# Expert gates of a two-layer hybrid block: the two parts of a token summed in PSUM by 128-column products

## The reference

```python
def peer_ffn(x, w_query, sub_keys, down, up):
    q = (xt @ w_query).reshape(T, H, 2, PEER_HALF)
    s = jnp.einsum('thcd,cnd->thcn', q, sub_keys).astype(jnp.float32)
    sv, si = lax.top_k(s, K)
    ...
    cand_i = (si[:, :, 0, :, None] * PEER_NKEYS + si[:, :, 1, None, :]).reshape(T, H, K * K)
    top_s, pos = lax.top_k(cand_s, K)
    idx = jnp.take_along_axis(cand_i, pos, axis=-1)
    gate = jax.nn.softmax(top_s, axis=-1)
```

## Time and profile before

| | us |
|---|---|
| median of three runs | 3004.24 |
| lowest and highest | 3000.68, 3005.28 |
| the profiled execution | 3001.47 |
| its span, from the first to the last instruction | 2999.7 |

### The profile page before, as it was taken

One profiled execution on the slowest core, in us unless ns is written; L12 is line 12 of the kernel. 1 busy time (PEld: TensorE's weight loads), 2 busy tenths in 40 slices (PEclk: granted clock), 3 DMA queues, 4 the chain that ended last, 5 costly groups with the idle time before them and its releaser, 6 DMA issues.

```text
span 2999.7 us, 43936 instructions
## 1 busy us (share of the span) xinstructions
PE 2936.4 (98%) x17304; PEld 2595.8 (87%) x17304; DVE 2015.1 (67%) x3109; ACT 1455.8 (49%) x2275; POOL 14.6 (0%) x37
## 2 busy tenths in 40 slices
PE   8999999999999899999999999999999999999998
PEld 6888888889999788888888999988898998888996
DVE  5869998765555586999876655557665556665554
ACT  5531775554444444257545444445455444545443
POOL 0000000000000000000000000000000000000000
PEclk9999999999999999999999999999999999999999
DMA  5334455765545433445567554545555655554553
GB/s 179 110 127 155 157 178 206 256 257 189 196 174 182 137 99 120 155 155 183 197 236 269 199 193 181 197 140 180 182 170 174 188 186 185 172 183 141 154 185 125
DMA packets 223246, 528.52 MB, mean 176 GB/s; under 512 B 13450, under 2 KB 87344, under 8 KB 212080
## 3 DMA queue, kind: packets, MB, share of 16 engines
q1 hardware_dynamic: 221856, 521.11, 50.9%
q0 software_dynamic: 1232, 5.25, 0.5%
HBM read 507.42 MB, written 18.88 MB: 175 GB/s over the span
## 4 chain that ended last, share of the span: by engine, by line
PE 93%; DVE 4%; ACT 1%; DMA 0%; issue 0%; SPq 0%; POOL 0%; DVEq 0%; ACTq 0%; POOLq 0%
PE ps L2235 16%; PE ps L1238 14%; PE ps L2219 12%; PE ps L1288 12%; PE ps L1301 12%; PE ps L1272 11%; PE ps L552 3%; PE ps L561 3%; PE ps L1227 2%; PE ps L2476 1%; DVE ring_lo L535 1%; PE ps L655 1%; PE ps L1050 1%; PE ps L2400 0%; PE ps L2384 0%; PE ps L1213 0%
## 5 line engine op out<-in xcount | busy, mean ns | idle before, releaser
L1886 DVE TENSOR_TENSOR ring_lo<-ring,w_hi 128x1024 fp32r<-128x1024 f32 x320 | 388.7, 1224 | 270.7 <-ACT w_hi L1882 269.5
L1882 ACT ACTIVATE w_hi<-ring 128x1024 fp32r<-128x1024 f32 x320 | 336.7, 1057 | 268.9 <-PE ps L2235 182.3
L1238 PE MATMUL ps<-h_t,ring 128*128 128x256 f32 x2048 | 463.5, 379 | 0.9 <-ACT arena L885 0.9
L1238 PEld LDWEIGHTS ps<-h_t,ring 128*128 128x128 f32 x2048 | 379.0, 190 | 47.5 <-issue 1.3
L1288 PE MATMUL ps<-h_t_lo,down_hi 128*128 128x256 f32 x1024 | 288.2, 281 | 0.0
L1288 PE MATMUL ps<-h_t_expert,down_lo 128*128 128x256 f32 x1024 | 287.8, 281 | 0.0
L1288 PE MATMUL ps<-h_t_expert,down_hi 128*128 128x256 f32 x1024 | 286.8, 280 | 0.0
L2219 PE MATMUL ps<-h_t_hi,w_hi 128*128 128x256 f32 x928 | 260.0, 280 | 2.7 <-ACT arena L2034 2.7
L2219 PE MATMUL ps<-h_t_lo,w_hi 128*128 128x256 f32 x928 | 261.4, 282 | 0.0
L2219 PE MATMUL ps<-h_t_hi,ring_lo 128*128 128x256 f32 x928 | 259.7, 280 | 0.0
L1673 DVE TENSOR_TENSOR up_lo<-ring,up_hi 128x2048 fp32r<-128x2048 f32 x64 | 146.7, 2292 | 99.8 <-ACT up_hi L948 99.8
(11 more groups left out here) (444 smaller groups left out, 6682.9 us busy)
## 6 DMA issues: line engine op xcount, KB each, us to landing
ring<-in_peer_down SPq DMA_DIRECT2D x128, 1024.0 KB, 5.0
ring<-in_w_in SPq DMA_DIRECT2D x140, 512.0 KB, 3.6
ring<-in_peer_up SPq DMA_DIRECT2D x68, 1024.0 KB, 4.7
ring<-in_w SPq DMA_DIRECT2D x132, 512.0 KB, 3.5
ring<-in_peer_up SPq DMA_DIRECT2D x120, 512.0 KB, 4.2
arena<-late_gates SPq DMA_DIRECT2D x16, 1024.0 KB, 6.5
ring<-in_w_out SPq DMA_DIRECT2D x16, 512.0 KB, 3.6
ring<-in_peer_w_query SPq DMA_DIRECT2D x16, 512.0 KB, 4.6
```

Of the source, the lines that this page charges most:

```text
L1238: m = pe.e.matmul(PS[:, act_bank(b), j * T:(j + 1) * T], RING[:, b % 2, j * D + kc * P:j * D + (kc + 1) * P], HT[:, kc, :], start=kc == 0, ...
L1882: a.e.activation(W_HI[:, g % HI_SLOTS, :], RAW[:, g % RAW_SLOTS, :], ACT.Copy).then_inc(*a.count(f"c{g}_hi"))
L1886: v.e.tensor_tensor(RAW_LO[:, g % RAW_SLOTS, :], RAW[:, g % RAW_SLOTS, :], W_HI[:, g % HI_SLOTS, :].bitcast(F32), ALU.subtract).then_inc(* ...
```

## The change

For each token `sums` makes two products of 128 columns into the same 128 columns of PSUM, the high part first (it starts the sum) and the low part onto it. The weights, HOT1 of the token, are the same in both. Four tokens now take one bank, and six banks take turns: GATE_BANKS = (0, 1, 2, 3, 6, 7). ScalarE copies the finished gates (`gates_high` is renamed `gates_out`, and it counts `gates{s}`); `gates_low` on VectorE is gone; whoever waited for `low` waits for `gates`, and a `sums` waits for the one six before.

```diff
-GATE_BANKS = (0, 2, 6)
+GATE_BANKS = (0, 1, 2, 3, 6, 7)
...
-        def gate_sums(s, part, late):
-
-            bank = GATE_BANKS[s % 3]
-            sums = PS[:, bank:bank + 2, :].rearrange("p b (j i n) -> p (b j) i n", i=2, n=P)
-            return sums[:, :, part, late * 64:(late + 1) * 64]
+        def gate_sums(s, late):
+
+            sums = PS[:, GATE_BANKS[s % 6], :].rearrange("p (j n) -> p j n", n=P)
+            return sums[:, :, late * 64:(late + 1) * 64]
...
-                a.e.activation(early_gates(s), gate_sums(s, 0, 0), ACT.Copy).then_inc(*a.count())
-                a.e.activation(late_of(s), gate_sums(s, 0, 1), ACT.Copy).then_inc(*a.count(f"high{s}"))
+                a.e.activation(early_gates(s), gate_sums(s, 0), ACT.Copy).then_inc(*a.count())
+                a.e.activation(late_of(s), gate_sums(s, 1), ACT.Copy).then_inc(*a.count(f"gates{s}"))
...
-                if s >= 3:
-                    pe.e.wait_ge(*pe.at(f"low{s - 3}"))
+                if s >= 6:
+                    pe.e.wait_ge(*pe.at(f"gates{s - 6}"))
                 for j in range(FEW):
-                    k, at = s % 2 * FEW + j, j % 2 * T
-                    m = pe.e.matmul(PS[:, bank + j // 2, at:at + T], HOT1[:, n % 2, k, :],
-                                    HOT2[n % 2][:, k, :, :].rearrange("p i n -> p (i n)"), start=True, stop=True)
+                    k = s % 2 * FEW + j
+                    for i in range(2):
+                        m = pe.e.matmul(PS[:, bank, j * P:(j + 1) * P], HOT1[:, n % 2, k, :], HOT2[n % 2][:, k, i, :],
+                                        start=i == 0, stop=i == 1)
                 m.then_inc(*pe.count(f"sum{s}"))
...
-            def gates_low(s):
-
-                v.e.wait_ge(*v.at(f"high{s}"))
-                v.e.tensor_tensor(early_gates(s), gate_sums(s, 1, 0), early_gates(s), ALU.add).then_inc(*v.count())
-                v.e.tensor_tensor(late_of(s), gate_sums(s, 1, 1), late_of(s), ALU.add).then_inc(*v.count(f"low{s}"))
-
...
-                if n >= 2:
-                    gates_low(2 * n - 4)
                 if n:
                     v.e.wait_ge(*v.at(f"hot_high{n - 1}"))
-                v.e.wait_ge(*v.mine(3 if n >= 2 else 1))
+                v.e.wait_ge(*v.mine(1))
...
-                if n >= 2:
-                    gates_low(2 * n - 3)
...
-            for s in range(SUMS - 4, SUMS):
-                gates_low(s)
-            v.e.wait_ge(*v.mine())
+            v.e.wait_ge(*v.at(f"gates{SUMS - 1}"))
...
-                        sp.e.wait_ge(*sp.at(f"low{2 * n + 1}"))
+                        sp.e.wait_ge(*sp.at(f"gates{2 * n + 1}"))
```

More of the change, by code:

```diff
@@ L915, in hot_high, with gates_out @@
                         .then_inc(*a.count(f"hot_high{n}" if j == GROUP - 1 else None))
-            def gates_high(s):
+            def gates_out(s):
                 if s // 2 >= STAGES and s % 2 == 0:
@@ L932, in hybrid_scalar @@
                 if n >= 2:
-                    gates_high(2 * n - 3)
+                    gates_out(2 * n - 3)
                     acts_out(2 * n - 3)
@@ L937, in hybrid_scalar @@
                 if n:
-                    gates_high(2 * n - 2)
+                    gates_out(2 * n - 2)
                     acts_out(2 * n - 2)
-            gates_high(SUMS - 1)
+            gates_out(SUMS - 1)
             for b in range(LEAD, HELD):
@@ L1217, in sums @@
             def sums(s):
-                n, bank = s // 2, GATE_BANKS[s % 3]
+                n, bank = s // 2, GATE_BANKS[s % 6]
                 if s % 2 == 0:
```

## The result

The changed kernel takes 3049.1 us (median of four runs, 3048.2 to 3053.5) where the kernel before took 3002.5 beside it: ratio 1.0155, 95% interval 1.0143 to 1.0168. It is slower by 46.6 us. The profiled execution took 3048.71 us with a span of 3046.9, 47.2 over the 2999.7 of before.

A forecast was written before the change was run, and what follows sets the result against it. The prediction took the gate stages to be bound by VectorE, by 0.4 us in 19.7, with TensorE right behind. Added pairs +54.3 less stalls 6.7 gave +47.6 us, forecast 3051 us; range 2994 to 3065, its own case 3043 to 3065.

The forecast's parts named there:

- The price of the added pairs: TensorE, each `sums`: eight load-and-product pairs at 112 ns, 0.896 us in place of 0.472, 0.424 us more.
- the 54.3 of the sum: TensorE, both gate stages: 128 `sums` with the added loads lie wholly on the path, +54.3 us.
- The stalls: TensorE, before every eighth `sums`: 16 waits of 0.42 us go once the VectorE additions are removed, 6.7 us less.
- VectorE itself has no hole: VectorE in the gate stage: its instructions run without a gap from 336.80 to 341.73, 4.93 us for eight tokens.
- bound by VectorE: Gate stage: VectorE needs 19.7 us for eight `sums`, TensorE 19.3, so VectorE binds by only 0.4 us.
- The figure of 4.93 us a group: VectorE in the gate stage: time for one group of eight tokens, 4 x 4.93 = 19.7 us for eight `sums`.
- A hidden load: Rival, TensorE `sums`: a pair costs by its columns, 59 ns, only the stalls go, 2997.5 us; chance 9%.
- a shorter one: Rival, TensorE `sums`: the load binds but a pair takes between 66 and 100 ns, 3024 us at 85 ns; chance 7%.
- The narrow fp32r product that loses its single pass: Rival, TensorE `sums`: each 128-column product costs two records of 108 ns, total time 3158 us; chance 16%.
- Work costed at nothing: Gate stages: ScalarE's evictions, TensorE's wait for `gates{s-6}`, late-gate DMA and the handover to the folds add no time.
- the 3.6 us expected: VectorE in the gate stage: a group falls from 4.93 to 3.6 us without the additions, under TensorE's 4.4.
- the 107 of the groups' busy time: VectorE, both stages: the removed additions L1619 and L1620 were 107 us busy, by which VectorE's busy time was to fall.

The follow-up runs named there:

- e2: Changed kernel with every product cut to 64 columns, high and low parts writing separate columns, nothing summed, eight loads kept: 3049.0 us, ratio 1.0147 to the kernel before.
- e3: Changed kernel with one 128-column product per token, the high part alone, four loads for eight: 2993.8 us, ratio 0.9965 to the kernel before.
- e4: Changed kernel with the low part's product weights cut to their first 64 columns, eight loads and products kept: 3025.4 us, ratio 1.0074 to the kernel before.
- e1: Kernel before without the gates_low additions on VectorE, its four 256-column products kept, low part left out of the result: 2996.9 us, ratio 0.9975.
- v2: Kernel before with the low part of one token in eight made by ScalarE, VectorE's L1644 cut to seven tokens: 3021.5 us, ratio 1.0054.

## Why the prediction was right

**The price of the added pairs.** 112 ns was taken from the rows of L1169 to L1171; it measured 111 ns, 0.89 us a `sums` for 0.896. That the load is what costs, argued then from the likeness of the records, is now shown by e2 (columns halved, nothing changes), e3 (single products, the same price) and e4 (weight columns halved, 61 ns). The added time can be read by itself: a stage of the changed kernel is 27.0 us longer than one of e1, which has neither the additions nor the added loads, 54.0 us in two for the 54.3 of the sum.

**The stalls.** 16 of 0.42 us, 6.7 us together, went; e1 measured 6.6 for them alone, 6.8 in its trace. The reading of their cause was wrong in one point: "VectorE itself has no hole" and "bound by VectorE". VectorE came 0.20 us late in every group, its own load is 4.73 us, and the pace was set by a circle through both engines: mask, `hot_high`, eviction, additions, mask. The earlier trace rows had a sign of it, 10.2 us of idle time before L1619: four long waits make 4.7 of them, and the rest is what such small holes add up to. The figure of 4.93 us a group was right, so the sum was not touched. But what v2's expectation built on the reading, that any relief of VectorE would do, was false, as v2 showed with 18 us. The change cut the circle by taking the additions out.

**The rivals.** A hidden load would have given 2.20 us a step, a shorter one less than 2.62; both are out. The narrow fp32r product that loses its single pass is out too: there are 1024 records, one for each product, a pair costs 111 ns and not 216, and in e4 the 128 columns pass in 61 ns.

**Work costed at nothing.** ScalarE's evictions kept their price (367 ns for 365) and gained idle time; the wait for `gates{s-6}` never shows; the folds at the stage's end started at 487.86 and ended before L1212 at 492.20. VectorE's own work in a group came out at the 3.6 us expected: 5.24 us a group less 1.62 of waiting. VectorE's total fell by 81 us, not by the 107 of the groups' busy time, since the records overlap: a 0.42 us addition stands only 0.33 after its neighbour.

**The total.** +54.3 - 6.7 = +47.6 was forecast; the spans differ by 47.2 and the medians by 46.6. Both terms hold by themselves (+54.0 and -6.8 in the stages), so the sum is not right by luck. The 3051 against 3049.1 holds mostly the median from which it started, 3004.24, where more runs gave 3002.5.

## What to carry to other kernels

Before a product is cut in two, count its weight loads: a pair of load and product cost 111 ns with 128 weight columns, whether the stream had 128 columns or 64, and one load under 256 columns cost 118. Work that rides along as more moving columns was nearly free, the same work as a product of its own was not. And where two engines wait for each other in turn, the pace is that of the whole circle even if one of them shows almost no idle time (here VectorE, 0.11 us a turn, while ScalarE showed 1.42): list the circle's members before work is moved between them, and try the order first.

## What the runs showed of the hardware

That an fp32r product needs no 256 columns for its single pass was not known from the rows of before: at 128 columns each left one record, and where a load of 64 columns let it, it took 61 ns, half of the 118 at 256. The price of a short pair fell with the weights' columns, 111 ns for 128 and 61 ns for 64; whether the 61 is still the load or already the stream, no run tells. A second load of the weights already in place was neither left out nor cheaper. Summing two products in the same PSUM columns cost nothing measurable at 111 ns a pair: the changed kernel and e2, which sums nothing, have the same step to 0.01 us.
